# Moving a one-hot selector from VectorE to ScalarE and respacing work between row gathers

## The reference

```
def block(args):                                  # 128 tokens at a time
    xc, ec, gc = args                             # features, expert numbers, gates
    u = jnp.take(expert_down, ec, axis=0)
    hdn = jax.nn.gelu(jnp.einsum('ted,td->te', u, xc))
    vsel = jnp.take(expert_up, ec, axis=0)
    return jnp.einsum('te,ted->td', gc * hdn, vsel)
```

## Time and profile before

| | |
|---|---|
| median of three runs | 3293.79 us |
| the profiled execution | 3294.96 us |
| its span in the profile | 3293.1 us |
| PE, DVE, ACT, POOL busy share | 87%, 65%, 33%, 20% |
| granted TensorE clock, mean | 0.93 |
| HBM read | 803.16 MB, 245 GB/s over the span |

### The profile page before, as it was taken

The page is one execution under the profiler, slowest core; times in us unless marked ns, Lnnn a source line. Parts: engine busy times, 40 slices in busy tenths (PEclk is TensorE's granted clock), DMA queues, the critical chain, the costliest instruction groups (busy, mean ns, idle before and its releaser), DMA issues.

```text
span 3293.1 us, 40692 instructions
## 1 busy us (share of the span) xinstructions
PE 2876.9 (87%) x15818; PEld 2410.4 (73%) x15818; DVE 2150.4 (65%) x3580; ACT 1073.0 (33%) x1654; POOL 663.9 (20%) x580
## 2 busy tenths in 40 slices
PE   3689999998989998799999989999987757999950
PEld 3689999996868987698888789888876645555520
DVE  6777777776765445534435557995579987665566
ACT  2133334334344444434334443011135546000000
POOL 5510000000000000000000001333435665334354
PEclk9689999998999999889989989999998879999975
DMA  8767787776856634455333444999987888999997
GB/s 292 245 234 247 259 273 265 255 255 202 289 185 173 167 103 130 127 147 173 103 103 103 141 154 142 354 317 403 399 316 233 280 281 274 404 405 397 406 334 247
DMA packets 359153, 807.97 MB, mean 245 GB/s; under 512 B 40120, under 2 KB 99776, under 8 KB 358192
## 3 DMA queue, kind: packets, MB, share of 16 engines
q1 hardware_dynamic: 284336, 497.89, 45.0%
q0 software_dynamic: 74624, 307.47, 26.0%
HBM read 803.16 MB, written 2.10 MB: 245 GB/s over the span
## 4 chain that ended last, share of the span: by engine, by line
PE 36%; DMA 19%; DVE 12%; ACT 3%; issue 3%; POOL 3%; DVEq 0%; ACTq 0%; POOLq 0%
DMA s<-in_up_rows,s 12%; PE ps L1825 10%; PE ps L1826 10%; PE ps L1827 10%; DMA s<-in_down_rows,s 8%; DVE s L1768 4%; POOL s L675 3%; DVE s L1790 2%; DVE ps L1735 1%; ACT s L1087 1%; PE ps L2203 1%; PE ps L2086 1%; ACT s L1090 1%; PE ps L2205 1%; DVE s L1641 1%
## 5 line engine op out<-in xcount | busy, mean ns | idle before, releaser
L1825 PE MATMUL ps<-r,r 128*128 128x256 f32 (+2 forms) x3248 | 1063.6, 327 | 78.0 <-DVE r L1140 45.5
L1826 PE MATMUL ps<-r,r 128*128 128x256 f32 (+2 forms) x3248 | 1044.7, 322 | 0.0
L1827 PE MATMUL ps<-r,r 128*128 128x256 f32 (+2 forms) x3248 | 1043.4, 321 | 0.0
L1140 DVE TENSOR_TENSOR r<-s,r 128x1024 fp32r<-128x1024 f32 (+1 forms) x532 | 648.4, 1225 | 575.6 <-ACT r L690 575.3
L690 ACT CAST r<-s 128x1024 fp32r<-128x1024 f32 (+1 forms) x532 | 550.8, 1040 | 898.3 <-PE ps L1827 851.2
L1825 PEld LDWEIGHTS ps<-r,r 128*128 128x128 f32 x3248 | 640.0, 197 | 135.8 <-DVE r L1140 43.0
L1826 PEld LDWEIGHTS ps<-r,r 128*128 128x128 f32 x3248 | 640.1, 197 | 43.1 <-issue 4.6
L1827 PEld LDWEIGHTS ps<-r,r 128*128 128x128 f32 x3248 | 639.3, 197 | 40.9
L1790 DVE SCALAR_TENSOR_TENSOR s<-s,s,s 128x1152 f32<-128x1152 f32 x256 | 362.9, 1418 | 192.7 <-DMA s<-in_up_rows,s 189.9
L1768 DVE CUSTOM_DVE_ANT_0 s<-s,s 128x1152 f32<-128x1152 f32 x256 | 345.7, 1355 | 118.7 <-DMA s<-in_down_rows,s 118.4
L675 POOL DMA_INDIRECT s<-in_down_rows,s x256 | 290.8, 1136 | 542.6 <-DVE s L1768 330.5
(11 more groups left out here) (281 smaller groups left out, 2419.1 us busy)
## 6 DMA issues: line engine op xcount, KB each, us to landing
s<-in_ada_w SPq DMA_DIRECT2D x192, 512.0 KB, 5.5
s<-in_ret_w_in SPq DMA_DIRECT2D x128, 512.0 KB, 5.4
s<-in_down_blocks SPq DMA_DIRECT2D x128, 448.0 KB, 6.6
s<-in_up_blocks SPq DMA_DIRECT2D x128, 448.0 KB, 6.6
s<-in_w_in SPq DMA_DIRECT2D x96, 512.0 KB, 3.8
s<-in_ret_w_in SPq DMA_DIRECT2D x128, 256.0 KB, 3.9
s<-in_ret_w_out SPq DMA_DIRECT2D x64, 512.0 KB, 5.5
s<-in_mla_w_in SPq DMA_DIRECT2D x48, 512.0 KB, 3.7
```

Of the source, the lines that this page charges most:

```text
L1140: v.tensor_tensor(lo_of(w), raw_of(w), hi_of(w).bitcast(F), ALU.subtract).then_inc(*lo_made.to(w))
L1825: pe.matmul(o, lh, rh, start=start, stop=False, skip_group_check=True)
L1826: pe.matmul(o, lh, rl, start=False, stop=False, skip_group_check=True)
L1827: return pe.matmul(o, ll, rh, start=False, stop=stop, skip_group_check=True)
```

## The change

Four things are edited. (1) For tile 0 the first selector is made on ScalarE: two instructions over 512 elements (distance, then one minus it, cut at zero), and four of 128 elements that multiply with the coefficient; VectorE's `first_ones` for tile 0 is gone. (2) The places of the picks: tile 0's are after rows 116 to 147, one a row (before: 146 to 161, two a row), tile 1's after rows 150, 153, ... 243 (before: 164, 166, 169, ... 241). `hidden(0)` and `coefficients(0)` are after rows 148 and 150. (3) Tile 1's first selectors are made after every second up row, 3 to 65 (before: after each of 2 to 33). (4) The second matmul of each compare has one row of contraction in place of 128: a row of ones against one row of the index table; ScalarE makes the row of ones once.

```diff
-        LESS = kept(128, of=arena_r)[0]
-        IDR, kept_end = kept(128, of=arena_r)
+        LESS, IDR = (kept(128, of=arena_r)[0] for _ in range(2))
+        ONER, kept_end = kept(128, of=arena_r)
...
-        first_hot = sig("first_hot", fours)
+        first_hot_a, first_hot_v = sig("first_hot_a", fours[0:32]), sig("first_hot_v", fours[32:])
...
-        PICK_AT = [146 + q // 2 for q in range(32)] + [164 + 5 * q // 2 for q in range(32)]
-        HOT_AT = [163 + 5 * (q + 3) // 2 for q in range(32)]
+        PICK_AT = [116 + q for q in range(32)] + [150 + 3 * q for q in range(32)]
...
-            s.copy(IDR, IDN).then_inc(*rounded.to(0))
+            s.copy(IDR, IDN)
+            s.copy(ONER, ONES).then_inc(*rounded.to(0))
...
             def first_tile(q):
-                o2 = flat(OH2[0])
+                o1, o2 = OH1[0], OH2[0]
                 if q < 32:
                     s.wait_ge(*compared.at((0, q)))
                     if q:
                         s.wait_ge(*built.at((0, q - 1)))
-                    s.activation(o2, bank[1], ACT.Abs).then_inc(*less_read.to((0, q)))
+                    s.activation(flat(o1), bank[0], ACT.Abs)
+                    s.activation(flat(o2), bank[1], ACT.Abs).then_inc(*less_read.to((0, q)))
                     s.wait_ge(*less_read.at((0, q)))
-                    s.activation(o2, o2, ACT.Relu, scale=-1.0, bias=1.0).then_inc(*second_hot.to((0, q)))
+                    s.activation(flat(o1), flat(o1), ACT.Relu, scale=-1.0, bias=1.0)
+                    s.activation(flat(o2), flat(o2), ACT.Relu, scale=-1.0, bias=1.0).then_inc(*second_hot.to((0, q)))
+                    s.wait_ge(*second_hot.at((0, q)))
+                    for k in range(4):
+                        c = 4 * q + k
+                        r = s.activation(o1[:, k, :], o1[:, k, :], ACT.Copy, scale=CFT[0][:, c:c + 1])
+                    r.then_inc(*first_hot_a.to((0, q)))
                 if q:
                     store(0, q - 1)
...
-                for q in range(32):
-                    if HOT_AT[q] == n:
-                        first_ones(0, q)
-                for q in range(64):
-                    if PICK_AT[q] == n:
-                        pick(*fours[q])
+                if n in PICK_AT:
+                    pick(*fours[PICK_AT.index(n)])
...
-                if 2 <= n < 34:
-                    first_ones(1, n - 2)
+                if n % 2 and n // 2 - 1 in range(32):
+                    q = n // 2 - 1
+                    if q == 0:
+                        v.wait_ge(*coef_copied.at(1))
+                    v.wait_ge(*built.at(fours[max(31, 30 + q)]))
+                    v.wait_ge(*compared.at((1, q)))
+                    v.scalar_tensor_tensor(out=OH1[q % 2], in0=bank[q % 2].rearrange("p (t i) -> p t i", t=4), scalar=0.0,
+                                           in1=CFT[1][:, 4 * q:4 * q + 4].unsqueeze(2).broadcast_to([128, 4, 128]),
+                                           op0=ALU.is_equal, op1=ALU.mult).then_inc(*first_hot_v.to((1, q)))
...
-                    r = pe.matmul(bank[b], IDR, LESS.unsqueeze(1).broadcast_to([128, 4, 128]), start=False, stop=True)
+                    r = pe.matmul(bank[b], ONER[0:1, :], LESS[0:1, :].unsqueeze(1).broadcast_to([1, 4, 128]), start=False, stop=True)
```

More of the change, by code:

```diff
@@ L1748, in coefficients @@
                 v.wait_ge(*coef_made.at(t))
[L1750 to L1760, removed]
             for n in range(256):
@@ L1771, in vector @@
                     gates((64, 100).index(n))
-                if n == 162:
+                if n == 148:
                     hidden(0)
-                if n == 164:
+                if n == 150:
                     coefficients(0)
-                for q in range(32):
-                    if HOT_AT[q] == n:
-                        first_ones(0, q)
-                for q in range(64):
-                    if PICK_AT[q] == n:
-                        pick(*fours[q])
+                if n in PICK_AT:
+                    pick(*fours[PICK_AT.index(n)])
             hidden(1)
@@ L2378, in compare @@
                               start=True, stop=False)
-                    r = pe.matmul(bank[b], IDR, LESS.unsqueeze(1).broadcast_to([128, 4, 128]), start=False, stop=True)
+                    r = pe.matmul(bank[b], ONER[0:1, :], LESS[0:1, :].unsqueeze(1).broadcast_to([1, 4, 128]), start=False, stop=True)
                 r.then_inc(*compared.to((t, q)))
                 for b, p in hs:
-                    free[b] = less_read.at((0, q)) if p else first_hot.at((t, q))
+                    free[b] = first_hot_v.at((1, q)) if t else less_read.at((0, q))
             def build_(t, q):
@@ L2386, in build_ @@
                 take(b)
-                pe.wait_ge(*first_hot.at((t, q)))
+                pe.wait_ge(*(first_hot_v if t else first_hot_a).at((t, q)))
                 pe.wait_ge(*second_hot.at((t, q)))
```

## The result

The changed kernel takes 3367.27 us (median of four runs, 3364.61 to 3368.22), against 3292.86 for the kernel before in the same sessions: 1.0226 times as long, with a 95% interval of 1.0208 to 1.0244. The prediction had 3322, within 3302 to 3345. The sign was right; of a loss of 74 us it had foreseen 28. The profiled execution took 3371.31 us, 4 us above the median.

A forecast was written before the change was run, and what follows sets the result against it. The prediction took VectorE's chain of 512 gathered rows as the bound. Down rows +33.7 and up rows -5.3 gave +28.4 us on the profiled 3293.1; with 1.9 around it and the profiled run 1.2 above median, 3322, range 3302 to 3345.

The forecast's parts named there:

- The wait at row 116: At tile 0's first pick VectorE would idle 58.0 us, until the first dense phase is done, with later rows queued behind.
- Tile 0's picks: From 2430.3, one pick and one row on VectorE at 2.40 us, 75.5 us for the stretch.
- a slow start: In tile 0's picks, 3.0 us added for TensorE starting at 1.2 GHz.
- The second selectors: Tile 1's selectors after every second up row would let rows before the second dense phase run at 2.08 us, not 2.22.
- the shift of the dense phase: The second dense phase would begin at 2877, 95 us later, and end at 3264, within its spare time.
- the up rows: Up rows outside the second dense phase would gain 5.3 us; the last would start at 3304.2.
- ScalarE's chain with 128 rows: In tile 1's picks, selector, build and compare take 5.9 us a group, 7.4 at 1.2 GHz, 6.4 mixed, ending before row 255.
- the eight rows of 1.86 us: Rows in the earlier trace read as having nothing between them, used as the lower bound of the row pace.
- The matmul with one row: In each compare, one row of contraction would be shorter by at most 0.4 us or cost the same; taken as zero.
- late chain: Rival: build, compare and selector are last in tile 1's picks; 7.4 us a group throughout gives 3349; chance 0.12.
- The rule about ScalarE: Skill's budget of about 0.3 us plus 0.83 ns an element per instruction: a group 6.8 us, time 3330; the prediction disagreed.

The follow-up runs named there:

- e1: The changed kernel with the second matmul of each compare back at 128 rows of contraction; 3324.5 us, ratio 1.0101.
- e12: The changed kernel with 64 rows of contraction in both matmuls of every compare; 3353.22 us, ratio 1.0174.
- e6: The changed kernel with 32 rows of 1/32 in the second matmul of each compare; 3368.72 us.
- e8: The kernel before with tile 1's selectors after every second up row and picks after rows 142 to 173 and 176 to 245; 3274.33 us, ratio 0.9951.

## Why the prediction was right and wrong

**The wait at row 116: right.** VectorE's wait at the first pick in the changed kernel:

```profile
DVE ps L1742 <- PE ps L2344: 62.9, 1, 62.9
```

62.9 us against 58.0. The row before it came 6.0 us sooner than in the trace of before, and the pick was ready 1.1 us sooner, which accounts for it. Tile 0's picks: rows 117 to 147 from 2430.3 to 2500.9, 2.35 us each; I had 2.40, and 3 us for a slow start that didn't come.

**The second selectors, the shift of the dense phase, the up rows: right.** With 128 rows the changed kernel (e1) has row 255 at 2727.4 (2727.0), the dense phase from 2876.7 to 3262.9 (2877 to 3264) and the last up row at 3304.3 (3304.2). That 2727.4 agrees so closely is luck, since two terms compensate: row 150 starts at 2504.1 (2511.7), and 105 rows take 223.4 us, 2.13 each, where I took 2.05. Two more do: from the last down row to the first up row it is 4.3 us and not 2.3, and the up rows take 572.6 us and not 574.9.

**ScalarE's chain with 128 rows: its parts right, the sum too small, and hidden by luck.** The prediction had 5.9 us a group at full clock and 7.4 at 1.2 GHz; e1 has 5.7 and, at its slowest, 7.47. But it mixed them by the mean clock of before into 6.4, and e1's mean is 6.92, since most groups have their build or their compare at 1.2 GHz. The chain began 7 us sooner than the 2517 worked out, and its last selector, at 2724.7, still came before the last down row; VectorE then waited 1.9 us for TensorE. One reading of the earlier trace rows was also off: among the eight rows of 1.86 us there stood one selector of 0.69 us, after row 248, so they were not rows alone.

**The matmul with one row: wrong, and this is the step that failed.** The prediction had "shorter by at most 0.4 us, or the same; I take zero". Measured, it is worth 42.8 us (3367.3 against e1's 3324.5). One group of tile 1's picks in the changed kernel, from selector to selector:

```profile
2657.84 0.60 ACT L1076 ACTIVATE s<-ps 128x512 f32<-128x512 f32 x1 [3.06 <-PE ps L2377]
2661.52 2.05 PE L2389 MATMUL ps<-s,s 128*128 128x128 f32 x8 [0.85 <-issue]
2663.22 0.77 PE L2375 MATMUL ps<-r 128*128 128x512 f32 x1
2663.92 0.79 PE L2377 MATMUL ps<-r 1*128 1x512 f32 x1
2664.64 0.80 PE L2375 MATMUL ps<-r 128*128 128x512 f32 x1
2665.37 0.79 PE L2377 MATMUL ps<-r 1*128 1x512 f32 x1
2666.20 0.60 ACT L1076 ACTIVATE s<-ps 128x512 f32<-128x512 f32 x1 [3.06 <-PE ps L2377]
```

ScalarE's selector is 3.6 us, as worked out. From the build's start at 2661.52 to the next selector at 2666.20 it is 4.68 us, where I had 2.07, and 3.58 as the upper end. Together 8.36, and 8.35 in the mean. TensorE's whole load is not what sets this: the last two groups, without a pick multiply, take 8.35 and 8.37 too, with TensorE waiting 3.7 us for the selector. Weight loads of the compare before this one show the part of alternation:

```profile
2655.57 0.28 PEld L2377 LDWEIGHTS ps<-r 1*128 1x128 f32 x1 [0.44 <-issue]
2656.29 0.29 PEld L2375 LDWEIGHTS ps<-r 128*128 128x128 f32 x1 [0.44 <-issue]
2657.01 0.28 PEld L2377 LDWEIGHTS ps<-r 1*128 1x128 f32 x1 [0.44 <-issue]
```

Each load is preceded by 0.44 us in which nothing is recorded that it waits for. In the kernel before, loads of this compare ran beside the matmul before them: the four matmuls started 0.57, 0.43 and 0.42 us apart at 1.2 GHz (from 2673.95 on). The same with 128 rows in e1 at 1.2 GHz:

```profile
2612.55 0.77 PE L2375 MATMUL ps<-r 128*128 128x512 f32 x1
2613.11 0.63 PE L2377 MATMUL ps<-r 128*128 128x512 f32 x1
2613.55 0.63 PE L2375 MATMUL ps<-r 128*128 128x512 f32 x1
2613.97 0.63 PE L2377 MATMUL ps<-r 128*128 128x512 f32 x1
```

0.56, 0.44, 0.42, and 1.85 for the compare; the changed kernel's 2.87 is 1.02 us more. The last group of e1 ran at a granted clock of 0.50 from one selector to the next:

```profile
2717.23 0.60 ACT L1076 ACTIVATE s<-ps 128x512 f32<-128x512 f32 x1 [3.42 <-PE ps L2377]
2724.70 0.60 ACT L1076 ACTIVATE s<-ps 128x512 f32<-128x512 f32 x1 [3.42 <-PE ps L2377]
```

That is 7.47 us with 128 rows. So I estimate that of the 8.35 about 0.9 us is the alternation, and 0.55, from 7.47 down to e1's mean of 6.92, the clock: over 31 groups some 27 and 17 us. In e12 the two changes that were left keep the group 0.29 above 7.47.

**Why I missed it.** The rival "late chain" had the place right and, for 128 rows, the price: 7.4 us a group at 1.2 GHz, against 7.47 in e1. It lacked the alternation's 0.9 us, and it had a chance of 0.12, since I took the clock of before as the clock to come. The cost of an operation that "nothing before has" was bounded by a duration alone, without its effect on the clock. There was a row near it in the trace of before that I did not read, the stretch of 32 matmuls with 16 rows of contraction just before the second dense phase. Here it stands with the two us ahead of it and the start of that phase:

```profile
2774.00:2776.00 2.00, 1.13 (x8) 0.96 (x9) 1.90 (x2) 0.92 (x2) 1.70 (x2) 1.00 0.51 205
2776.00:2782.00 6.00, 5.98 (x32) 5.79 (x32) 2.99 (x3) 0.00 (x0) 4.32 (x4) 0.60 0.94 275
2782.00:2786.00 4.00, 4.00 (x7) 1.93 (x7) 3.38 (x3) 0.00 (x0) 1.31 (x2) 0.50 0.96 339
```

TensorE is busy 5.98 of 6 us and the granted clock falls, to 0.60 in the mean and 0.50 behind it. The clock fell while TensorE was fully busy. The cause is not shown: it may be the 16 rows, or the idle time just before, for from 2772 to 2776 TensorE was busy 1.95 of 4 us. As a warning it was reason to give the rival more than 0.12, and a higher end to the range.

**The rule about ScalarE** (the Trainium skill, ScalarE: Activation LUTs, Rules for kernel authors) would have had 1.62 us for the four narrow instructions; after the change they took 1.28 (2660.14), so the sum disagrees with the trace as it did before. The rule is for one instruction whose bias is a pointer; the prediction added it up four times without overlap, and applied it to the 512-wide ones too, whose scale and bias are plain numbers. The Trainium skill (TensorE: Matmul & The Clock Gate, Why this matters for your kernels) says that a single matmul with 32 rows of contraction takes as long as with 128. Between matmuls of 128 rows it does not here: in e6, with 32 rows, the compare takes 2.87 us at 1.2 GHz (2655.44 to 2658.31) against 1.85 with 128. By that rule, carried over to one row, the edit was free.

## What to carry to other kernels

Don't shrink the contraction of a matmul that sits among full ones to save work: here, at 1, 32 and 64 rows, it saved no time, cost the overlap of the weight loads, and left TensorE at half its clock in a stretch where it was hardly ever idle. When a chain through several engines may become the longest part, price it at both clocks and not at the mean: the stretches at 1.2 GHz can fall just on the chain, as they did in e1. Read the granted clock beside the busy share; a busy share that rises while the clock is 0.50 is work that got slower. And when instructions are placed by a count, compare the time at which the counted event comes with the time at which the data is ready: here the first pick could not be ready before 2429, so the row after which it stands should be one that ends then (142 in e8), not one that ends 63 us earlier.

## What the hardware showed that I had not expected

With the same work, 32 or 64 rows of contraction in one of two compare matmuls gave a granted clock of 0.50 and 0.51 over 180 us with TensorE busy 90% and 89%, 128 rows gave 0.78 to 0.81 with it busy 64 to 65%, and zeros in 127 of the 128 rows changed nothing (0.81). A matmul with one row was recorded with 0.49 us at 2.4 GHz where that with 128 rows had 0.39, and the loads around it no longer ran beside a matmul.
